# Two token tiles interleaved column by column in every activation buffer of a decoder trunk

## The reference

```
for i in range(DEPTH):                       # 2
    xn = rmsnorm(h, g_mix[i])
    h = h + (attn_mixer(xn, ...) if i % 2 == 0 else rglru_mixer(xn, ...))
    h = h + swiglu(rmsnorm(h, g_ffn[i]), w_ffn_gate[i], w_ffn_up[i], w_ffn_down[i])
    gate = sigmoid(rmsnorm(h, g_ple[i]) @ w_ple_gate[i])
    h = h + gate * (p[i] @ w_ple_proj[i])
return rmsnorm(h, g_final)
```

## Time and profile before

| | |
|---|---|
| time, median of 3 runs | 2373.56 us (2373.51 to 2375.59) |
| time of the profiled execution | 2373.45 us |
| its span (first to last instruction) | 2371.7 us |
| TensorE busy / weight loads busy | 2353.1 us (99%) / 1948.8 us (82%) |
| VectorE busy | 1566.8 us (66%) |
| ScalarE busy | 1143.5 us (48%) |

### The profile page before, as it was taken

How to read it: one execution, slowest core, us unless ns; L and a number is a source line. 1 busy time by engine, 2 the same in 40 slices (tenths; PEclk the granted TensorE clock), 3 DMA queues, 4 the chain that set the end, 5 groups by cost and what they waited for, 6 DMA issues and landing times.

```text
span 2371.7 us, 29398 instructions
## 1 busy us (share of the span) xinstructions
PE 2353.1 (99%) x10768; PEld 1948.8 (82%) x10768; DVE 1566.8 (66%) x2212; ACT 1143.5 (48%) x1482; POOL 8.5 (0%) x31
## 2 busy tenths in 40 slices
PE   9999999999999999999999999999999999999998
PEld 7888778888888888888888888888888888888887
DVE  5556678676676676666597777866676676666656
ACT  5435555544444444444454575544444444444455
POOL 0000000000000000000000000000000000000000
PEclk9999999999999999999999999999999999999999
DMA  6844536666666666666568455566666666566664
GB/s 191 281 134 116 147 121 205 187 193 195 194 188 197 192 193 194 193 193 193 185 194 264 127 160 183 190 194 192 191 193 194 194 187 198 192 194 195 194 207 151
DMA packets 241195, 443.86 MB, mean 187 GB/s; under 512 B 16680, under 2 KB 30800, under 8 KB 240976
## 3 DMA queue, kind: packets, MB, share of 16 engines
q1 hardware_dynamic: 240768, 442.23, 61.1%
q10 hardware_dynamic: 336, 0.41, 0.0%
HBM read 440.49 MB, written 2.10 MB: 187 GB/s over the span
## 4 chain that ended last, share of the span: by engine, by line
PE 95%; DVE 2%; ACT 2%; issue 1%; DMA 0%; SPq 0%; ACTq 0%; DVEq 0%
PE ps L1527 30%; PE ps L1529 30%; PE ps L1528 30%; PE ps L1754 1%; PE ps L1479 1%; ACT w_hi L651 1%; DVE w_lo L949 1%; ACT prob L862 0%; DVE prob L1295 0%; PE ps L1664 0%; PE ps L1677 0%; DMA h<-in_x_dram 0%; PE ps L1659 0%; PE ps L1702 0%; ACT junk L719 0%
## 5 line engine op out<-in xcount | busy, mean ns | idle before, releaser
L949 DVE TENSOR_TENSOR w_lo<-raw,w_hi 128x1024 fp32r<-128x1024 f32 x820 | 998.5, 1220 | 738.8 <-ACT w_hi L651 733.2
L651 ACT ACTIVATE w_hi<-raw 128x1024 fp32r<-128x1024 f32 x820 | 862.8, 1055 | 1023.3 <-PE ps L1529 1002.9
L1527 PE MATMUL ps<-w_hi,xa_hi 128*128 128x512 f32 x1664 | 647.7, 389 | 0.0
L1529 PE MATMUL ps<-w_hi,xa_lo 128*128 128x512 f32 x1664 | 647.4, 389 | 0.0
L1528 PE MATMUL ps<-w_lo,xa_hi 128*128 128x512 f32 x1664 | 647.3, 389 | 0.0
L1527 PEld LDWEIGHTS ps<-w_hi,xa_hi 128*128 128x128 f32 x1664 | 312.4, 188 | 64.9
L1529 PEld LDWEIGHTS ps<-w_hi,xa_lo 128*128 128x128 f32 x1664 | 312.4, 188 | 64.8
L1528 PEld LDWEIGHTS ps<-w_lo,xa_hi 128*128 128x128 f32 x1664 | 312.4, 188 | 64.5
L1527 PE MATMUL ps<-w_hi,xb_hi 128*128 128x512 f32 x864 | 349.8, 405 | 0.2 <-DVE w_lo L949 0.2
L1529 PE MATMUL ps<-w_hi,xb_lo 128*128 128x512 f32 x864 | 337.4, 391 | 0.0
L1528 PE MATMUL ps<-w_lo,xb_hi 128*128 128x512 f32 x864 | 336.8, 390 | 0.0
(11 more groups left out here) (242 smaller groups left out, 1017.2 us busy)
## 6 DMA issues: line engine op xcount, KB each, us to landing
raw<-in_w_ffn_gate_dram SPq DMA_DIRECT2D x176, 512.0 KB, 4.4
raw<-in_w_ffn_up_dram SPq DMA_DIRECT2D x176, 512.0 KB, 4.3
raw<-in_w_ffn_down_dram SPq DMA_DIRECT2D x176, 512.0 KB, 4.6
raw<-in_w_in_attn_dram SPq DMA_DIRECT2D x88, 512.0 KB, 3.7
raw<-in_w_ple_gate_dram SPq DMA_DIRECT2D x64, 512.0 KB, 4.6
raw<-in_w_in_rec_dram SPq DMA_DIRECT2D x64, 512.0 KB, 4.1
raw<-in_w_out_attn_dram SPq DMA_DIRECT2D x32, 512.0 KB, 3.8
raw<-in_w_out_rec_dram SPq DMA_DIRECT2D x32, 512.0 KB, 3.8
```

The lines of the kernel that those rows point to most:

```text
L651: nc.scalar.activation(w_hi[:, s, 0:n], raw[:, s, 0:n], ACT.Copy).then_inc(hi_ready, 1)
L949: nc.vector.tensor_tensor(w_lo[:, s, 0:n], raw[:, s, 0:n], w_hi[:, s, 0:n].bitcast(F32), ALU.subtract).then_inc(lo_ready, 1)
L1527: nc.tensor.matmul(o, xh[:, k, tok], w_hi[:, s, wk], start=(k == 0), stop=False)
L1529: ins = nc.tensor.matmul(o, xl[:, k, tok], w_hi[:, s, wk], start=False, stop=(k == nkt - 1))
```

## The change

The order of the 256 columns in a k-tile's row is changed in all those buffers: column 2t + m now holds token t of tile m. The row is still 1,024 bytes. The helpers that the diff adds are views: `by_token` reads or writes an interleaved row tile by tile, `rows_of` gives a row in the plain order the same shape, `of_tile` is one tile's 128 columns (every second one, 8 bytes apart), `slot_of` is where a 32x32 block goes in `sg`. What was one contiguous access of 256 elements is now two runs of 128 elements with a step of 8 bytes.

```
...
+        def by_token(t):
+            return t.rearrange("p (t m) -> p m t", m=NT)
+        def rows_of(t):
+            return t.rearrange("p (m t) -> p m t", m=NT)
+        def of_tile(t, m):
+            return by_token(t)[:, m]
+        def slot_of(t, a):
+            return t.rearrange("p k (t m) -> p k m t", m=NT)[:, :, :, 32 * a:32 * a + 32]
...
-                        o = dst[0][:, k0 + 2 * b + f, :] if isinstance(k0, int) else \
-                            dst[0][:, bass.ds(k0 + (2 * b + f), 1), :]
-                        src = ps[:, bank + b, f * S:(f + 1) * S]
+                        o = by_token(dst[0][:, k0 + 2 * b + f, :])
+                        src = rows_of(ps[:, bank + b, f * S:(f + 1) * S])
...
-                    nc.scalar.activation(X["B"][0][:, 4 * g:4 * g + 4], xc[:, 4 * g:4 * g + 4], ACT.Copy
-                                         ).then_inc(r_hi, 1)
+                    for f in range(4 * g, 4 * g + 4):
+                        ins = nc.scalar.activation(by_token(X["B"][0][:, f]), rows_of(xc[:, f]), ACT.Copy)
+                    ins.then_inc(r_hi, 1)
...
                 for a in range(4):
-                    ins = nc.vector.transpose(dst[:, :, :, 32 * a:32 * a + 32], src[32 * a:32 * a + 32])
+                    ins = nc.vector.transpose(slot_of(dst, a), src[32 * a:32 * a + 32])
...
-                        nc.tensor.matmul(o, w_hi[:, s, wk], xh[:, k], start=(k == 0), stop=False)
+                        nc.tensor.matmul(o, w_hi[:, s, wk], by_token(xh[:, k]), start=(k == 0), stop=False)
...
-                        nc.tensor.matmul(o, xh[:, k, tok], w_hi[:, s, wk], start=(k == 0), stop=False)
-                        nc.tensor.matmul(o, xh[:, k, tok], w_lo[:, s, wk], start=False, stop=False)
-                        ins = nc.tensor.matmul(o, xl[:, k, tok], w_hi[:, s, wk], start=False,
+                        nc.tensor.matmul(o, of_tile(xh[:, k], m), w_hi[:, s, wk], start=(k == 0), stop=False)
+                        nc.tensor.matmul(o, of_tile(xh[:, k], m), w_lo[:, s, wk], start=False, stop=False)
+                        ins = nc.tensor.matmul(o, of_tile(xl[:, k], m), w_hi[:, s, wk], start=False,
                                                stop=(k == nkt - 1))
...
```

More of the change, by code:

```diff
@@ L770, in run_chunk @@
                         for layer in range(2):
-                            ins = nc.scalar.activation(
-                                pT_hi[:, layer], ps[:, EX + layer, :].rearrange("p (k t) -> p k t", k=2), ACT.Copy)
+                            for k in range(2):
+                                ins = nc.scalar.activation(by_token(pT_hi[:, layer, k]),
+                                                           rows_of(ps[:, EX + layer, k * S:(k + 1) * S]), ACT.Copy)
                         ins.then_inc(p_hi, 1)
@@ L1003, in turn_split @@
                     for f in range(2):
[L1004 to L1008, removed]
+                        hi, lo = (by_token(dst[z][:, k0 + 2 * b + f, :]) for z in range(2))
+                        src = rows_of(ps[:, bank + b, f * S:(f + 1) * S])
                         if gain is None:
@@ L1022, in turn_tiles @@
                 src = rows.rearrange("p m (k d) -> p k m d", k=4)[:, :, :, 32 * c:32 * c + 32]
-                dst = sgT[32 * c:32 * c + 32].rearrange("p k (m t) -> p k m t", m=NT)
+                dst = sgT[32 * c:32 * c + 32]
                 for a in range(4):
-                    ins = nc.vector.transpose(dst[:, :, :, 32 * a:32 * a + 32], src[32 * a:32 * a + 32])
+                    ins = nc.vector.transpose(slot_of(dst, a), src[32 * a:32 * a + 32])
                 if c == 3:
@@ L1133, in run_chunk @@
                         for layer in range(2):
-                            ins = nc.vector.tensor_tensor(
-                                pT_lo[:, layer], ps[:, EX + layer, :].rearrange("p (k t) -> p k t", k=2),
-                                pT_hi[:, layer].bitcast(F32), ALU.subtract)
+                            for k in range(2):
+                                ins = nc.vector.tensor_tensor(
+                                    by_token(pT_lo[:, layer, k]), rows_of(ps[:, EX + layer, k * S:(k + 1) * S]),
+                                    by_token(pT_hi[:, layer, k].bitcast(F32)), ALU.subtract)
                         ins.then_inc(p_ready, 1)
@@ L1434, in griffin @@
                     dve.wait_ge(r_hi, g + 1)
-                    nc.vector.tensor_tensor(X["B"][1][:, t4], xc[:, t4], X["B"][0][:, t4].bitcast(F32),
-                                            ALU.subtract).then_inc(r_lo, 1)
+                    for f in range(4 * g, 4 * g + 4):
+                        ins = nc.vector.tensor_tensor(by_token(X["B"][1][:, f]), rows_of(xc[:, f]),
+                                                      by_token(X["B"][0][:, f].bitcast(F32)), ALU.subtract)
+                    ins.then_inc(r_lo, 1)
             dve.wait_ge(vec_turned, 1)
@@ L1512, in multiply_slot @@
                 if q.kinds[r].name == "gates":
-                    o = ps[0:NGATE, 2 * r, 0:S]
+                    o = rows_of(ps[0:NGATE, 2 * r, 0:S])
                     for k in range(k0, k0 + nk):
                         wk = slice((k - k0) * w, (k - k0 + 1) * w)
-                        nc.tensor.matmul(o, w_hi[:, s, wk], xh[:, k], start=(k == 0), stop=False)
-                        nc.tensor.matmul(o, w_lo[:, s, wk], xh[:, k], start=False, stop=False)
-                        ins = nc.tensor.matmul(o, w_hi[:, s, wk], xl[:, k], start=False, stop=(k == nkt - 1))
+                        nc.tensor.matmul(o, w_hi[:, s, wk], by_token(xh[:, k]), start=(k == 0), stop=False)
+                        nc.tensor.matmul(o, w_lo[:, s, wk], by_token(xh[:, k]), start=False, stop=False)
+                        ins = nc.tensor.matmul(o, w_hi[:, s, wk], by_token(xl[:, k]), start=False, stop=(k == nkt - 1))
                     ins.then_inc(w_used, 1)
@@ L1524, in multiply_slot @@
                     for k in range(k0, k0 + nk):
-                        tok = slice(m * P, (m + 1) * P)
                         wk = slice((k - k0) * w, (k - k0 + 1) * w)
-                        nc.tensor.matmul(o, xh[:, k, tok], w_hi[:, s, wk], start=(k == 0), stop=False)
-                        nc.tensor.matmul(o, xh[:, k, tok], w_lo[:, s, wk], start=False, stop=False)
-                        ins = nc.tensor.matmul(o, xl[:, k, tok], w_hi[:, s, wk], start=False,
+                        nc.tensor.matmul(o, of_tile(xh[:, k], m), w_hi[:, s, wk], start=(k == 0), stop=False)
+                        nc.tensor.matmul(o, of_tile(xh[:, k], m), w_lo[:, s, wk], start=False, stop=False)
+                        ins = nc.tensor.matmul(o, of_tile(xl[:, k], m), w_hi[:, s, wk], start=False,
                                                stop=(k == nkt - 1))
```

## The result

The changed kernel takes 2438.42 us (median of 4 runs, 2437.7 to 2442.48) against 2373.77 before: 64.7 us more, a ratio of 1.0275 with a 95% interval of 1.0263 to 1.0287. The forecast was no change.

The account below looks back on a forecast made before the run. The prediction took TensorE's pace to bound the kernel: 9,792 matmuls at 226.7 ns, 2,220 us of the 2371.7 us span. All terms were put at 0, giving 2373.6 us, range 2369.5 to 2384.

Parts of the forecast that it names:

- Step 1: The 9,792 stationary loads, now with a step of 8 bytes: hidden behind matmuls with 115 ns left, so cost 0.
- "faster" rival: TensorE's 512-column matmuls: another load walk frees some of 13.4 ns each; all of it 131 us, 2242 us. Chance 0.03.
- The first rival: Strided weight loads outlast the matmul pace, 231.4 ns each, and set it: 46 us more, 2420 us. Chance 0.10.
- Step 2: Moving reads of 48 gate matmuls, now in two 8-byte-step runs: taken as 0, at most 5.5 us.
- Step 3: Strided reads and writes on DVE and ACT (transposes, roundings, subtractions): at most 0.24 us each, hidden, taken as 0.
- Step 4: Instructions split at L915, L1435 and the embedding: 1.5 us at a step on ACT and DVE together, hidden, 0.
- the lead: How far ahead of TensorE the ring of four slots has weights ready: about 5.6 us, hiding added ACT and DVE work.
- The second rival: DVE becomes the bound in output projections and first embedding, its strided instructions 0.24 us dearer: 9 us, 2383 us. Chance 0.07.

## Why the prediction was wrong, step by step

- **The bound** was read rightly: the time followed TensorE's pace, 94% of the span before.
- **Step 1 is the step that failed**, in the sentence that the load "leaves 115 ns" and that TensorE slows only when it is used up. The margin was right: the strided load by itself is 118 ns against 111, and more than 100 are still spare. What was wrong is that a hidden load costs nothing. In these float32r streams the pace of 226.7 ns was measured only with the full, contiguous load, at a matching place of the moving operand's 256-byte period. Elsewhere it was mostly 230 to 234, and with the step of 8 bytes so at every place, 233.3 at the kernel's own. The term I put at 0 was 60.5 us.
- **The row that should have warned me was misread.** The earlier trace rows shows one 24-column load beside one 512-column matmul. I took it for "load and matmul do not take cycles from each other". A stream of such pairs runs at 232 ns. One matmul says nothing of the steady state of a stream, and a step read as 0.23 us cannot tell 227 ns from 232.
- **The excess of 226.7 over 213.3 ns** stood in the "faster" rival as a collision of the two reads in SBUF, with a chance of 0.03 and only as a gain. It looked in the right place, with the other sign: a layout that moves the reads can make the excess larger as well as smaller. I did not price that side. Whether it is a collision in the memory no run shows.
- **The first rival** (2420 us) is nearest in time and wrong in kind for 8 bytes: the load does not reach the pace. Its bound came close for a larger step: 111 + 120 = 231 ns was forecast for a penalty on every column, and a load with a step of 16 bytes measures 233, which binds, 2455.87 us in the kernel. That the forecast of 2420 lies nearest to 2438.42 is luck.
- **Step 2** failed too, by less: I took 0 and named 5.5 us as the upper bound. Measured 4.8 us, at 229 ns a matmul: the value lay close to the upper bound.
- **Step 3** was right: 1 ns on VectorE's instructions, 14 on ScalarE's, and no new wait of TensorE behind them (its share of the chain is 95% still). **Step 4** too: four L1451 instructions of 420 ns in place of one of 1219 made 0.5 us, inside the lead. The second rival falls with them.
- **The note on SBUF cachelines in the Trainium skill** (SBUF — State Buffer) says that two accesses in a 16-byte line suffice. For the load alone the streams nearly agree: 111 ns contiguous, 118 with 8 bytes, 233 with 16. For the moving side they don't: 8 bytes halve the pace, 114 to 229 ns. And it gives no rule for a load and a moving read together, which is what decided here.

What stays open: whether it is a conflict in SBUF and which, why a load of 2 columns (231 ns at place 0) does not get the best pace, why the step of 8 bytes reaches it at none of the sixteen places, and what chooses between two paces at one place. The runs show that place and step move the pace, not by what arrangement of the memory.

## What to carry to other kernels

Before a layout change, ask what pace the full TensorE stream has over its ideal, and whether that excess depends on where the operands lie; here one added constant of 64 bytes costs as much as striding every tile. A hidden load is free only while it does not change the pace of the matmul that hides it, so price a changed load by a stream of the changed pair, not by the slack beside it. With float32r operands, keep both at the same place of 256 bytes, the stationary tile contiguous and full, and the moving side contiguous: there a step of 8 bytes doubled the time.

## What was not expected of the hardware

- Relative place alone moves a 512-column float32r stream between 226.7 and 234 ns, and left a bfloat16 stream of 512 columns and a float32 one of 256 where they were (215.8, at 0 and 64 bytes).
- The losses over the columns' own time (one a cycle at 2.4 GHz, granted clock 1.00) come near multiples of 6.7 ns: 13.3 (226.7 and, with 384 columns, 173.3 against 160), 20 (233.3 and, with 448 columns, 206.7 against 186.7), and 6.7 (113.3 against 106.7 with 24 stationary and 256 moving columns). With 496 columns it is 16.7 (223.4), so this is a pattern and no rule.
- Some places have two paces, and a phase of hundreds of microseconds keeps the one it falls into (234 and 230 ns for the same instructions).
- A moving read in contiguous pairs of float32 (8 of every 16 bytes) is as slow as single ones 8 bytes apart: 230 and 227 ns for 256 columns.
- A stationary load with a step of 16 bytes takes 233 ns for 128 columns, twice a contiguous one, and shows in its recorded duration (310 against 188 ns).
- Those 233 ns do not follow TensorE's clock. In three streams with only 64 moving columns the granted clock was 0.50, the level of 1.2 GHz. There the contiguous load (L101) takes (10.39 - 0.40) / 47 = 213 ns, twice its 111 at clock 1.00, and so does the step of 8 bytes; the step of 16 bytes (L105) takes (11.37 - 0.42) / 47 = 233 ns, as at clock 1.00:

```profile
190.52 10.39 PE L101 MATMUL ps<-W,A 128*128 128x64 f32 x48
...
210.97 11.37 PE L105 MATMUL ps<-W,A 128*128 128x64 f32 x48
```

```profile
190.50:200.50 10.00, 10.00 (x48) 10.00 (x49) 0.00 (x0) 0.00 (x0) 0.00 (x0) 0.50 0.01 2
...
211.00:221.90 10.90, 10.90 (x48) 10.90 (x49) 0.00 (x0) 0.00 (x0) 0.00 (x0) 0.50 0.00 0
```
